# Rotary embedding in four pieces of heads, its single steps placed between the weight subtractions

## The reference, cut to what matters

```python
h = rms_norm(x, norm1_g) * (1 + sc1) + sh1
proj = h @ w_in                                   # (256, 7424)
qa, ka, va, qb, kb, vb, gl = jnp.split(proj, IN_SPLITS, axis=-1)
qa = rope(rms_norm(qa.reshape(b, s, DIL_HEADS, HEAD_DIM), qn_a), positions)   # 12 heads of 64
ka = rope(rms_norm(ka.reshape(b, s, DIL_HEADS, HEAD_DIM), kn_a), positions)   # 12 heads
qb = rms_norm(qb.reshape(b, s, DIFF_HEADS, 2, HEAD_DIM), qn_b)                # 16 heads
kb = rms_norm(kb.reshape(b, s, DIFF_HEADS, 2, HEAD_DIM), kn_b)                # 16 heads
q1, q2 = rope(qb[:, :, :, 0], positions), rope(qb[:, :, :, 1], positions)
k1, k2 = rope(kb[:, :, :, 0], positions), rope(kb[:, :, :, 1], positions)
gates = jax.nn.sigmoid(gl + b_gate)

def rope(x, positions):
    ang = positions[:, :, None, None] * inv_freq
    cos, sin = jnp.cos(ang), jnp.sin(ang)
    x1, x2 = x[..., : hd // 2], x[..., hd // 2:]
    return jnp.concatenate([x1 * cos - x2 * sin, x2 * cos + x1 * sin], axis=-1)
```

## Time and profile before

| | us |
|---|---|
| median of 3 runs (lowest, highest) | 2128.17 (2126.04, 2130.38) |
| the profiled execution, its own time | 2135.76 |
| its span, first to last instruction | 2132.9 |
| mean granted TensorE clock | 0.923 |
| TensorE busy | 1873.9 (88%) |
| VectorE busy | 1362.5 (64%) |
| ScalarE busy | 911.1 (43%) |
| GpSimd busy | 87.0 (4%) |

### The profile page before, as it was taken

One profiled execution on the slowest core, in us unless ns is written; L12 is line 12 of the kernel. 1 busy time (PEld: TensorE's weight loads), 2 busy tenths in 40 slices (PEclk: granted clock), 3 DMA queues, 4 the chain that ended last, 5 costly groups with the idle time before them and its releaser, 6 DMA issues.

```text
span 2132.9 us, 25755 instructions
## 1 busy us (share of the span) xinstructions
PE 1873.9 (88%) x10004; PEld 1610.2 (75%) x10004; DVE 1362.5 (64%) x1848; ACT 911.1 (43%) x951; POOL 87.0 (4%) x101
## 2 busy tenths in 40 slices
PE   1897895688979989999999999979987779999997
PEld 0676774467869867999999999878966568878875
DVE  5458767655889855555555555556854368887885
ACT  1354423231123334444444444445533346666664
POOL 0000100000000033111000000000000000000000
PEclk9898956698989999999999999989987879999999
DMA  6543342341325477666655555544335148898892
GB/s 233 197 177 125 131 151 108 127 158 63 141 103 177 163 244 235 205 214 203 215 179 194 179 195 180 194 162 161 118 120 196 51 162 330 321 347 330 325 349 114
DMA packets 60590, 403.91 MB, mean 189 GB/s; under 512 B 7921, under 2 KB 8337, under 8 KB 14049
## 3 DMA queue, kind: packets, MB, share of 16 engines
q1 hardware_dynamic: 50976, 370.17, 47.4%
q0 software_dynamic: 5808, 20.29, 3.3%
q10 hardware_dynamic: 3730, 12.42, 1.7%
HBM read 390.79 MB, written 12.06 MB: 189 GB/s over the span
## 4 chain that ended last, share of the span: by engine, by line
PE 79%; DVE 13%; ACT 4%; issue 3%; DMA 2%; DVEq 0%; ACTq 0%; SPq 0%
PE ps L1944 20%; PE ps L1945 20%; PE ps L1946 20%; PE ps L2022 6%; PE ps L2257 3%; DVE wlo L1032 2%; ACT whi L582 2%; DMA raw<-in_stream_dram 2%; PE ps L2106 1%; PE ps L2430 1%; PE ps L2085 1%; PE ps L2495 1%; PE ps L2316 1%; PE ps L1968 1%; DVE H L1058 1%
## 5 line engine op out<-in xcount | busy, mean ns | idle before, releaser
L1032 DVE TENSOR_TENSOR wlo<-raw,whi 128x2048 fp32r<-128x2048 f32 x186 | 425.7, 2291 | 432.8 <-ACT whi L582 432.8
L582 ACT ACTIVATE whi<-raw 128x2048 fp32r<-128x2048 f32 x186 | 356.2, 1916 | 461.5 <-PE ps L1946 418.2
L1944 PE MATMUL ps<-thi,whi 128*128 128x256 f32 x1088 | 311.1, 286 | 5.1 <-DVE tlo L1044 4.2
L1945 PE MATMUL ps<-tlo,whi 128*128 128x256 f32 x1088 | 310.3, 285 | 0.0
L1946 PE MATMUL ps<-thi,wlo 128*128 128x256 f32 x1088 | 310.1, 285 | 0.0
L1944 PE MATMUL ps<-whi,thi 128*128 128x512 f32 (+1 forms) x584 | 236.4, 405 | 32.8 <-DVE wlo L1032 25.7
L1944 PE MATMUL ps<-whi,phi 128*128 128x512 f32 x608 | 243.1, 400 | 21.4 <-DVE plo L1508 15.0
L1945 PE MATMUL ps<-wlo,phi 128*128 128x512 f32 x608 | 241.1, 396 | 0.0
L1946 PE MATMUL ps<-whi,plo 128*128 128x512 f32 x608 | 240.0, 395 | 0.0
L1945 PE MATMUL ps<-wlo,thi 128*128 128x512 f32 (+1 forms) x584 | 231.1, 396 | 0.0
L1946 PE MATMUL ps<-whi,tlo 128*128 128x512 f32 (+1 forms) x584 | 230.9, 395 | 0.0
(11 more groups left out here) (374 smaller groups left out, 2685.8 us busy)
## 6 DMA issues: line engine op xcount, KB each, us to landing
raw<-in_stream_dram SPq DMA_DIRECT2D x272, 1024.0 KB, 4.8
BIG<-in_stream_dram SPq DMA_DIRECT2D x80, 1024.0 KB, 7.1
BIG<-g_spill POOLq DMA_DIRECT2D x64, 128.0 KB, 4.6
g_spill<-H ACTq DMA_DIRECT2D x4, 1024.0 KB, 4.8
g_spill<-MOD ACTq DMA_DIRECT2D x4, 1024.0 KB, 4.9
MID<-in_gains_dram POOLq DMA_DIRECT2D x7, 512.0 KB, 4.6
s_spill<-MOD ACTq DMA_DIRECT2D x10, 256.0 KB, 4.8
MOD<-in_b_ada_dram POOLq DMA_DIRECT2D x1, 2048.0 KB, 13.6
```

Of the source, the lines that this page charges most:

```text
L582: nc.scalar.activation(whi[:, u % 2, :], raw[:, u % 2, :], ACT.Copy).then_inc(unit_hi, 1)
L1032: nc.vector.tensor_tensor(wlo[:, u % 2, :], raw[:, u % 2, :], whi[:, u % 2, :].bitcast(f32), ALU.subtract).then_inc(unit_split, 1)
L1944: nc.tensor.matmul(out, ahi, bhi, start=start, stop=False)
L1945: nc.tensor.matmul(out, ahi, blo, start=False, stop=False)
```

## The change

- `ROPES` names four pieces: (tile 0, heads 0 to 23), (tile 1, heads 0 to 23), (tile 0, heads 24 to 55), (tile 1, heads 24 to 55). Squares, sums, means, roots and all products are now done for one piece at a time. Pieces 0 and 1 need only blocks 0 to 2 of proj.
- The scratch space `rots` has two places, columns 0 and 2048 of MID, which the pieces use in turn. The squares of piece 2 wait for `rope_done` of piece 0, those of piece 3 for piece 1.
- VectorE's steps are five functions (`qk_means`, `qk_normed`, `qk_turned`, `qk_cosine`, `qk_roped`), and nearly always one subtraction stands between two of them. The set-up steps are spread likewise from unit 2 on. The loops over units 2 to 9 on both engines are written out.
- ScalarE's sines and exponential stand behind block 1 (before: behind block 4), the squares of pieces 0 and 1 behind block 2, those of 2 and 3 behind blocks 6 and 7, the roots behind blocks 3, 5, 7 and 10.
- `rope_done` now counts to 4. TensorE's program is otherwise the same, and so are SyncE's and GpSimd's.

The diff, cut to its core:

```diff
+        ROPES = ((0, 0, 24), (1, 0, 24), (0, 24, QK_HEADS), (1, 24, QK_HEADS))
+        rots = [mid[:, at:at + (b - a) * HD].rearrange("p (h d) -> p h d", d=HD)
+                for at, (_, a, b) in zip((0, 2048, 0, 2048), ROPES)]
...
 (ScalarE)
+            def squares(k):
+                t, a, b = ROPES[k]
+                nc.scalar.activation(rots[k], proj[:, t, a * HD:b * HD].rearrange("p (h d) -> p h d", d=HD),
+                                     ACT.Square).then_inc(qk_sq, 1)
+            def roots(k):
...
+                act.wait_ge(qk_ms, k + 1)
+                nc.scalar.activation(stat, stat, ACT.Sqrt).then_inc(qk_std, 1)
+            in_block(0)
+            in_block(1)
             act.wait_ge(angles_ready, 1)
             nc.scalar.activation(sin, ang, ACT.Sin).then_inc(sincos_ready, 1)
             nc.scalar.activation(cos, atmp, ACT.Sin).then_inc(sincos_ready, 1)
             act.wait_ge(lam_dots, 1)
             nc.scalar.activation(lam2, lam2, ACT.Exp).then_inc(lam_exp, 1)
+            in_block(2)
+            act.wait_ge(acc_free, 2 * 3)
+            squares(0)
+            squares(1)
+            in_block(3)
+            roots(0)
+            in_block(4)
             in_block(5)
+            roots(1)
             in_block(6)
             act.wait_ge(acc_free, 2 * (QK_W // 512))
-            squares(0)
-            roots(0)
+            act.wait_ge(rope_done, 1)
+            squares(2)
             in_block(7)
+            act.wait_ge(rope_done, 2)
+            squares(3)
+            roots(2)
             in_block(8)
-            in_high(20)
-            act.wait_ge(rope_done, 1)
-            squares(1)
-            in_high(21)
-            in_out(9)
-            roots(1)
-            for b in range(10, 13):
-                in_block(b)
+            in_block(9)
+            in_block(10)
+            roots(3)
+            in_block(11)
+            in_block(12)
             in_block(13)
...
 (VectorE, behind the set-up)
+            lo_in(8)
+            qk_means(0)
+            lo_in(9)
+            qk_normed(0)
+            lo_in(10)
+            qk_turned(0)
+            lo_in(11)
+            qk_cosine(0)
+            lo_in(12)
+            qk_roped(0)
+            qk_means(1)
+            lo_in(13)
+            qk_normed(1)
...
+            lo_in(26)
+            qk_roped(3)
+            lo_in(27)
+            lo_in(28)
             dve.wait_ge(gate_biased, TT)
...
 (TensorE)
-            pe.wait_ge(rope_done, TT)
+            pe.wait_ge(rope_done, len(ROPES))
```

More of the change, by code:

```diff
@@ L630, in _ @@
             tr_high(T_H1)
[L633 to L638, removed]
             def in_high(k):
@@ L1130, in _, with lo_in @@
             tr_low(T_H1)
[L1133 to L1142, removed]
+            def lo_in(k):
+                lo(U_IN + k)
+            lo_in(2)
             dve.wait_ge(rows_loaded, 16 * 5)
@@ L1204, in _, with qk_stats @@
             kinds = ((0, 12), (12, 24), (24, 40), (40, 56))
[L1205 to L1213, removed]
-                mark(nc.vector.tensor_tensor(rows, rows, stat.unsqueeze(2).broadcast_to([P, QK_HEADS, HD]), ALU.mult))
-                in_block((7, 10)[t])
-                settle()
-                for k, (a, b) in enumerate(kinds):
+            def qk_stats(k):
+                t, a, b = ROPES[k]
+                return qk_stat[:, t * QK_HEADS + a:t * QK_HEADS + b]
@@ new lines, in qk_rows, with qk_kinds, qk_means @@
+            def qk_rows(k):
+                t, a, b = ROPES[k]
+                return proj[:, t, a * HD:b * HD].rearrange("p (h d) -> p h d", d=HD)
+            def qk_kinds(k):
+                _, first, end = ROPES[k]
+                return [(n, a - first, b - first) for n, (a, b) in enumerate(kinds) if first <= a and b <= end]
+            def qk_means(k):
+                stat = qk_stats(k)
+                dve.wait_ge(qk_sq, k + 1)
+                nc.vector.tensor_reduce(stat, rots[k], axis=AX.X, op=ALU.add).then_inc(qk_summed, 1)
+                dve.wait_ge(qk_summed, k + 1)
+                nc.vector.tensor_scalar(stat, stat, 1.0 / HD, EPS, ALU.mult, ALU.add).then_inc(qk_ms, 1)
@@ L1218, in _, with qk_normed, qk_turned @@
+            def qk_normed(k):
+                stat, rows = qk_stats(k), qk_rows(k)
+                dve.wait_ge(qk_std, k + 1)
+                mark(nc.vector.reciprocal(stat, stat))
+                settle()
+                mark(nc.vector.tensor_tensor(rows, rows, stat.unsqueeze(2).broadcast_to([P, rows.shape[1], HD]), ALU.mult))
+            def qk_turned(k):
+                rows = qk_rows(k)
+                settle()
+                for n, a, b in qk_kinds(k):
                     for out_h, in_h in ((0, hf32), (hf32, 0)):
-                        table = rope_s[:, t, k, out_h:out_h + hf32].unsqueeze(1).broadcast_to([P, b - a, hf32])
@@ L1223, in _, with qk_roped @@
                 settle()
-                for k, (a, b) in enumerate(kinds):
-                    table = rope_c[:, t, k, :].unsqueeze(1).broadcast_to([P, b - a, HD])
+                for n, a, b in qk_kinds(k):
+                    table = rope_c[:, ROPES[k][0], n, :].unsqueeze(1).broadcast_to([P, b - a, HD])
                     mark(nc.vector.tensor_tensor(rows[:, a:b, :], rows[:, a:b, :], table, ALU.mult))
-                if t:
-                    in_block(12)
+            def qk_roped(k):
+                rows = qk_rows(k)
@@ L1229, in _ @@
                 settle()
[L1230 to L1234 removed]
+                nc.vector.tensor_tensor(rows, rows, rots[k], ALU.add).then_inc(rope_done, 1)
+            lo_in(8)
[6 more added lines that the diff above has]
+            qk_cosine(0)
@@ new lines, in _ @@
+            lo_in(12)
[3 more added lines that the diff above has]
+            qk_normed(1)
+            lo_in(14)
+            qk_turned(1)
+            lo_in(15)
+            qk_cosine(1)
+            lo_in(16)
+            qk_roped(1)
+            lo_in(17)
+            qk_means(2)
+            lo_in(18)
+            qk_normed(2)
+            lo_in(19)
+            qk_turned(2)
+            lo_in(20)
+            qk_cosine(2)
+            lo_in(21)
+            qk_roped(2)
```

37 lines of the change are left out of this document (19 added, 18 removed).

## The result

Five runs of each kernel: 2126.04 us before (2124.73 to 2130.38), 2108.88 us after (2107.33 to 2115.43). The ratio is 0.9916, with a 95% interval of 0.9899 to 0.9933: a gain of 17.2 us by the medians and of 14 to 21 by the interval, where the forecast was 20.4 and its time 2107.8.

A forecast was written before the change was run, and what follows sets the result against it. TensorE bounds the kernel, busy 88%, but waits for VectorE's weight subtractions in the w_in product. Terms 125.1 + 0.5 + 0.6 + 8.7 + 0.4 make 135.3 us against 155.7: gain 20.4 off median 2128.17, 2107.8; range 2098 to 2119.

The forecast's parts named there:

- unit 6: One of w_in's weight units 0 to 28; ScalarE's table loads and small activations delay its copy: 0.5 us lost.
- slot: VectorE's free time between two weight subtractions, 3.15 us; with 0.95 slack, a step up to 4.1 costs nothing.
- 5.44 us rhythm: TensorE's undisturbed time per weight unit in the w_in product, from two subtraction starts; expected unbroken between 103 and 160.
- the 3.6 us one: VectorE's largest slot, holding piece 0's addition and piece 1's means: over 3.15 but under 4.1, so no stall.
- Unit 18: Weight unit whose ScalarE copy waits behind the root for piece 2's means: 0.6 us lost after slack.
- Unit 24: Weight unit whose VectorE subtraction GpSimd's two b_gate additions hold up: 7.1 us waiting plus 1.6 at the lower clock.
- The last addition: Piece 3's addition ends the rotary embedding at about 223 us, before TensorE's last unit ends, so it delays nothing.
- Rival B: GpSimd's additions cost TensorE little or nothing, so 8.7 us comes back: 2099 us; chance 0.15.
- C: ScalarE copies wait behind a root or Square for VectorE at two of four pieces: loss 11, 2119 us; chance 0.15.
- D: Weight loads slow to 10.4 us, each costing 3.1; at ten loads 10.6 us more, 2139; chance 0.04.
- E: VectorE's order did not set the end, so no gain: within 0.2% of 2128 us; chance 0.04.
- B's bounds: Limits for the additions' cost: 0 if they meet idle time or single-input sums, 8.9 + 2.9 if nothing gets between.

The follow-up runs named there:

- whole-tile experiment: Kernel before with the changed kernel's set-up and one subtraction between two steps, but pieces left as whole tiles of 56 heads: 2112.0 us, ratio 0.9918.
- eight-piece run: Changed kernel with GpSimd's two b_gate additions cut into eight of 512 columns, each issued when its block and tile are evacuated: 2102.2 us, ratio 0.9873.
- the last run: Changed kernel with additions in eight pieces, bias loads in twelve, and the sines and the root of piece 2 moved: 2096.0 us, ratio 0.9847.

## Why the prediction was right

By its steps:

1. The set-up is hidden, and unit 6 pays for ScalarE's table loads: 0.5 us forecast, 0.37 measured. With the loads moved, the subtraction of unit 6 is done 3.6 us early, and the set-up alone is worth 4.0 us of the stage. A table load took 1.28 us with the next instruction right behind it, as in the rows of before.
2. No slot of its own length stalls TensorE: right, the 5.44 us rhythm holds through all slots of pieces 0 and 1, the 3.6 us one included. The whole-tile experiment shows the other side of the same sum: with steps of 3.9 to 4.4 us every slot from unit 16 on costs 0.25 to 1.74 us. The added instructions are ten, not the "some 25" of the prediction (VectorE's count goes from 1848 to 1858), so they take 1.6 us and not 4; neither is on the path.
3. Unit 18: 0.6 forecast, 0.32 measured, and gone with the root moved behind the copy.
4. Unit 24: 7.1 us of waiting and 1.6 at the lower clock forecast, 6.65 and six matmuls 0.2 us slower measured. One instruction of VectorE got in between the two additions, as in the earlier trace rows. The experiment without them shows that they are the cause, the one with eight pieces that the length of one addition is what counts. The prediction says that products and additions both read proj and MID; by the earlier trace rows the products read proj and MOD and write MID, so proj alone is read by both. The times that it gives at units 16 to 24 are also about 1 us later than its own sum makes them (unit 24 at 102.38 + 0.5 + 0.6 + 18 x 5.44 = 201.4 and not 202.3), those of VectorE about as much, so that the waits hardly change by it. The slow matmuls behind one and the same wait of about 6.65 us were 6, 11 and 12 in three runs, 1.4 to 2.6 us, so this term is known only to a microsecond.
5. The last addition is done at 223.8, forecast 223; nothing waited for it.

The sum was 20.4 us for the stage and the stage gave 19.9. The stretch that the sum is made for, from the wait of unit 6 on, took 134.9 us where it says 135.3. In this, two small errors meet: the named waits and slow matmuls came to 8.7 us and not 9.8, and the first matmuls behind the waits with the tail to 1.0 and not 0.4. Ahead of that stretch 0.9 us were lost: unit 5's wait grew from 2.89 to 3.42 us, and there was one more slow matmul at the start.

The time is nearer than the sum deserves. The forecast of 2107.8 starts from a median of 2128.17, and the five runs gave 2126.04 for the kernel before. So the kernel before came out 2.1 us under the starting point and the gain, 17.2 us by the medians, 3.2 under the forecast; the two cancel in part, and that the time is hit within 1.1 us is luck. The stage's 19.9 lies inside the interval of 14 to 21, and what makes the medians' 17.2 less isn't shown.

What the prediction did not have is that unchanged stretches differ between executions, above all the memory stretch, 6.4 us by its clock. It took the distance of 7.6 us between the profiled execution of before and the median for the spread of the runs, without asking where; that execution had the longer form. The forecast did not suffer, because the gain was worked out inside the stage and then taken off the median.

Rival B fell with unit 24's wait, C with the absence of other waits, D since TensorE waited for no load but unit 5's, E with the time. One piece of the reasoning for B's bounds was too simple: VectorE can also keep the additions out for a long time (last section). In the whole-tile run they came in beside the last units, and TensorE's two waits there were 0.90 and 0.86 us.

## What to carry to other kernels

Where one engine prepares data for another in a fixed rhythm, work out the free time of a slot once (here 3.15 us, and 0.95 of slack that is there only once in a row of full slots) and cut all side work to fit it; the order of the pieces mattered little after that in the one other order that was run. Then look for the instructions of a third engine that shut the preparing engine out: their single length has to fit the slot as well. And a large transfer of another queue can be cut to pieces that the stream's own slack covers, as the bias loads were. Before two single profiles are subtracted, compare them stretch by stretch: the unchanged ones show what the difference holds beside the change.

## What the runs showed of the hardware

GpSimd's additions and VectorE's instructions with two SBUF inputs exclude each other for a whole instruction. The Trainium skill says so (SBUF — State Buffer, "Who interferes with whom"), and the traces agree. An addition takes 2.17 ns a column, 4.4 us for 2048 columns and 1.1 for 512, and a VectorE instruction with two inputs that met it took up to 4.4 us more in the one case and up to 1.1 in the other. Instructions with one input were not held up: a sum beside an addition took 2.28 us in the eight-piece run, as it does alone.

The traces also show when an addition gets in. Fifteen pairs of additions stand in the nine traces that have them. In twelve the first addition got in at the end of the VectorE instruction that was running when it was issued; each time that was the first with two inputs behind a pause or behind an instruction with one input. In seven of the twelve VectorE's next instruction had one input, so only five of them say anything. Issued deeper in an unbroken row the addition stayed out until the row ended: the third pair of the eight-piece run for 2 us (until 189.36), the same pair of the last run likewise, and in the whole-tile run for 16 us. This is read from the traces and was not tested by itself.

The memory stretch has two lengths, 32.7 and 39.1 us, with granted clocks of 0.85 and 0.66 (the levels of 2.4 and 1.2 GHz in other shares), for the same instructions. TensorE pauses there 1.2 to 2.4 us between short groups. What decides the form is open. The code of the stretch is the same in all ten, and the two profiled executions with the longer form lay 7.6 and 4.4 us above the medians of their kernels, which speaks against the kernel as the cause; but there is one profile of each. So 6.4 us of a difference between two single executions may be this.

The number of slow matmuls behind a pause varies too: behind the same wait at unit 24 it was 6, 11 and 12 in three traces, at the start of the stage 7 to 14.
